# A bidirectional scan in 32-token chunks: odd chunks' halves swapped, both directions in one phase, PSUM banks in changing roles

## The reference, cut to what matters

```python
def step(S, inp):
    rt, wt, kt, vt, at, bt = inp
    Sa = jnp.einsum('zbhij,zbhj->zbhi', S, at)
    S = S * wt[..., None, :] + Sa[..., :, None] * bt[..., None, :] + vt[..., :, None] * kt[..., None, :]
    return S, jnp.einsum('zbhij,zbhj->zbhi', S, rt)
...
_, ys = lax.scan(step, S0, xs)
y = (ys[:, 0] + ys[::-1, 1]).transpose(1, 0, 2, 3)
```

## Time and profile before

| | |
|---|---|
| median of 3 runs | 1479.38 us (1470.05 to 1479.9) |
| the profiled execution | 1478.97 us, span 1477.2 us |
| mean granted TensorE clock | 0.96 of 2.4 GHz |
| TensorE busy | 1368.8 us, 93% of the span |
| DVE busy | 878.4 us, 59% |
| ACT busy | 562.9 us, 38% |
| first L893 of the scan to the last L950 | 340.5 to about 642 us |
| L784 | from 92.8 to 277 us |

### The profile page before, as it was taken

One profiled execution on the slowest core, in us unless ns is written; L12 is line 12 of the kernel. 1 busy time (PEld: TensorE's weight loads), 2 busy tenths in 40 slices (PEclk: granted clock), 3 DMA queues, 4 the chain that ended last, 5 costly groups with the idle time before them and its releaser, 6 DMA issues.

```text
span 1477.2 us, 28497 instructions
## 1 busy us (share of the span) xinstructions
PE 1368.8 (93%) x11292; PEld 1092.4 (74%) x11292; DVE 878.4 (59%) x1151; ACT 562.9 (38%) x825; POOL 168.9 (11%) x165
## 2 busy tenths in 40 slices
PE   6999999985898998878978899999999998999996
PEld 2487787874787877756866688888888887888885
DVE  4967767896565676756248755555555563323235
ACT  3725525311565675672114333333333342112121
POOL 1000100220010000021100322222222200000000
PEclk9999999996899998989988999999999999999998
DMA  5046856974566575621410222222222256322113
GB/s 198 19 121 173 199 138 161 219 219 94 147 211 206 152 219 151 184 70 44 156 71 0 86 85 85 85 78 73 80 81 73 84 172 241 114 86 92 46 33 114
DMA packets 154404, 179.51 MB, mean 122 GB/s; under 512 B 61264, under 2 KB 116624, under 8 KB 154352
## 3 DMA queue, kind: packets, MB, share of 16 engines
q1 hardware_dynamic: 141184, 152.69, 35.3%
q10 hardware_dynamic: 9264, 14.19, 3.1%
q0 software_dynamic: 3904, 11.93, 2.6%
HBM read 121.16 MB, written 57.54 MB: 121 GB/s over the span
## 4 chain that ended last, share of the span: by engine, by line
PE 74%; DVE 13%; ACT 5%; DMA 3%; issue 3%; POOL 1%; ACTq 1%; SPq 1%; DVEq 0%; POOLq 0%
PE banks L1041 26%; PE banks L667 16%; PE banks L649 6%; PE banks L1076 4%; PE banks L655 3%; DVE work L1815 2%; DVE work L1811 2%; PE banks L893 2%; PE banks L903 2%; PE banks L926 2%; PE banks L784 2%; DMA work<-in_w_in 2%; PE banks L631 1%; ACT work L1274 1%; PE banks L872 1%
## 5 line engine op out<-in xcount | busy, mean ns | idle before, releaser
L1041 PE MATMUL banks<-op,sw_hi 128*128 128x512 f32 x1176 | 363.6, 390 | 5.2 <-DVE hT L1997 3.5
L1041 PEld LDWEIGHTS banks<-op,sw_hi 128*128 128x128 f32 x1176 | 221.4, 188 | 52.0 <-DVE sw_lo L1610 3.9
L1041 PE MATMUL banks<-op,sw_lo 128*128 128x512 f32 x588 | 229.3, 390 | 0.0
L1947 DVE TENSOR_TENSOR xT<-xT,banks 128x1024 f32<-128x1024 f32 x24 | 29.3, 1221 | 168.3 <-PE banks L667 156.6
L1041 PEld LDWEIGHTS banks<-op,sw_lo 128*128 128x128 f32 x588 | 110.8, 188 | 23.0
L1384 ACT ACTIVATE sw_hi<-work 128x1024 fp32r<-128x1024 f32 (+1 forms) x63 | 75.9, 1204 | 123.8 <-PE banks L1041 111.7
L1610 DVE TENSOR_TENSOR sw_lo<-work,sw_hi 128x1024 fp32r<-128x1024 f32 (+1 forms) x63 | 90.1, 1430 | 39.4 <-ACT sw_hi L1384 39.3
L649 PE MATMUL banks<-ph_hi,pw_hi 128*128 128x512 f32 x272 | 86.8, 401 | 6.4 <-DVE pw_lo L1610 4.0
L649 PE MATMUL banks<-ph_hi,pw_lo 128*128 128x512 f32 x272 | 85.2, 395 | 0.0
L667 PE MATMUL banks<-g_hi,down_hi 128*128 128x512 f32 x256 | 79.6, 393 | 4.4 <-DVE g_lo L1610 4.3
L667 PE MATMUL banks<-g_lo,down_hi 128*128 128x512 f32 x256 | 79.5, 392 | 0.0
(11 more groups left out here) (246 smaller groups left out, 2578.3 us busy)
## 6 DMA issues: line engine op xcount, KB each, us to landing
work<-scan_d SPq DMA_DIRECT2D x32, 768.0 KB, 4.8
work<-in_w_gu SPq DMA_DIRECT2D x88, 256.0 KB, 4.6
scan_d<-work SPq DMA_DIRECT2D x16, 1024.0 KB, 5.6
g_d<-hT SPq DMA_DIRECT2D x22, 512.0 KB, 2.9
scan_d<-work SPq DMA_DIRECT2D x32, 256.0 KB, 6.3
work<-in_w_down SPq DMA_DIRECT2D x16, 512.0 KB, 3.7
work<-in_w_in ACTq DMA_DIRECT2D x15, 512.0 KB, 3.8
work<-g_d SPq DMA_DIRECT2D x15, 512.0 KB, 4.5
```

The costliest lines, as they stand in the source:

```text
L1041: mm = pe.matmul(banks[:, 3 * slot + bank, :], w[:, n, k * P:(k + 1) * P], x[n][:, k, :], start=(opens and k == 0 and p_ == 0), stop=(k == ...
```

## The change

**Odd chunks' halves are swapped.** `half_rows(e, odd)` gives partitions 64 (e xor odd) on. For odd chunks the keys, the gram rows, the v rows and U of head e lie in the other half. The gram matmul of an odd chunk writes across, and chunks alternate between `ps[1]` and `ps[2]`. In DRAM the rows are stored in the swapped order; the stores of v become 8 DMAs of 32 tokens' partitions for each head pair instead of 2.

**Phases merged.** In the first part of X, in U, the state product and Y, the loops are now j, then z, then e, with one wait ahead and one increment behind, so that four matmuls in a row lie in four quadrants of the array. The second part of X keeps z outside.

**Banks.** In even steps XY are banks 0, 1 and US 2, 3; in odd steps the other way round. The first part of X now waits for `S_add` (the previous state product read), U waits for `Y_out`, the previous Y copied.

**Evictions merged.** U's low half (DVE), its high half (ACT), Y's copy, the add and the multiply by `PC` take both directions in one instruction of 512 columns. `PC` of direction 1 is kept in the order of the steps.

**The order of attention's work.** On TensorE, odd steps have two groups of transposes behind X, the third and the first value product behind U, and the other two value products behind Y. On DVE the logits are spread: head 0 behind the even step's U copy, head 1 behind its state update, heads 2 and 3 behind the odd step's X copy; the maxima stand behind the odd step's state update. On ACT the X copy goes ahead of the fourth exponential; of the normalisation one head stands behind U and three behind Y's copy in the even step; `attended` and three exponentials stand behind Y's copy (and behind the squaring, in late steps) of the odd step.

```diff
+        def half_rows(e, odd, at=0, n=64):
+            first = 64 * (e ^ odd) + at
+            return slice(first, first + n)
...
+        def u_rows(slot, rows, cc):
+            return UV[slot].rearrange("p z c j i -> p (z c) (j i)")[rows, cc:4 - cc:3 - 2 * cc, :]
...
-                    sp.dma_start(v_d.rearrange("(b p) n -> p b n", p=P)[:, :, bass.ds((e * NPAIR + j) * HD, HD)],
-                                 vts[:, :, HD * e:HD * e + HD]).then_inc(s["v_stored"], 16)
+                    for m in range(P // C):
+                        tokens, at = slice(C * m, C * m + C), ((e ^ m % 2) * NPAIR + j) * HD
+                        sp.dma_start(v_d.rearrange("(b p) n -> p b n", p=P)[tokens, :, at:at + HD],
+                                     vts[tokens, :, HD * e:HD * e + HD]).then_inc(s["v_stored"], 16)
...
-                        out = ps[1 + c // 16][h, (c % 16) * 64:(c % 16) * 64 + 64]
+                        out = ps[1 + c % 2][half_rows(e, c % 2), (c // 2) * 64:(c // 2) * 64 + 64]
...
+                    XY = [banks[:, 2 * cc + z, 0:NPAIR * HD] for z in range(2)]
+                    US = [banks[:, 2 - 2 * cc + z, :] for z in range(2)]
...
-                    for z in range(2):
-                        c2 = cc if z == 0 else 1 - cc
-                        pe.wait_ge(sz[z]["U_e0"], n + 1)
-                        pe.wait_ge(sz[z]["U_e1"], n + 1)
-                        settled()
-                        for j in range(NPAIR):
+                    pe.wait_ge(s["U_low"], n + 1)
+                    pe.wait_ge(s["U_high"], n + 1)
+                    settled()
+                    for j in range(NPAIR):
+                        for z, c2 in enumerate(c2s):
                             for e in range(2):
-                                h = slice(64 * e, 64 * e + 64)
-                                mm = pe.matmul(US[z][h, 256 + j * HD:256 + (j + 1) * HD],
-                                               BKs[slot][h, z, j, c2 * HD:c2 * HD + HD], UV[slot][h, z, c2, j, :],
+                                mm = pe.matmul(US[z][64 * e:64 * e + 64, 256 + j * HD:256 + (j + 1) * HD],
+                                               BKs[slot][half_rows(e, c2), z, j, c2 * HD:c2 * HD + HD],
+                                               UV[slot][half_rows(e, c2), z, c2, j, :],
                                                start=True, stop=True)
-                        mm.then_inc(sz[z]["S_mm"], 1)
+                    mm.then_inc(s["S_mm"], 1)
...
+                        act.wait_ge(X_mm[1], n + 1)
+                        act.activation(Xs[:, 1], banks[:, 2 * cc + 1, 0:256], ACT.Copy).then_inc(X_out[1], 1)
                         if cc == 0 and behind:
                             exponentials(blk - 1, 1 - g, (3,))
...
+                        act.activation(Ys[q % 2][:, :, :], banks[:, 2 * cc:2 * cc + 2, 0:256], ACT.Copy).then_inc(s["Y_out"], 1)
                         if late and q in (1, 2):
                             y_square(2 * i + (q - 1 - 2 * YT), q - 1)
+                        if cc == 0 and behind:
+                            normalised(blk - 1, 1 - g, (1, 2, 3))
+                        if cc == 1:
+                            if behind:
+                                attended(*((i, 0) if g else (i - 1, 1)))
+                            act.wait_ge(s["nm_ready"], blk + 1)
+                            exponentials(blk, g, (0, 1, 2))
...
+                        dve.wait_ge(s["S_mm"], n + 1)
+                        tt(St[:, :, :, :], S[:, :, :, :], banks[:, 2 - 2 * cc:4 - 2 * cc, 256:512]
+                           .rearrange("p z (j i) -> p z j i", j=NPAIR), ALU.add).then_inc(s["S_add"], 1)
+                        dve.wait_ge(s["S_add"], n + 1 + FREE)
+                        tt(S[:, :, :, :], St[:, :, :, :], PC[:, :, :, bass.ds(n, 1)].broadcast_to([P, 2, NPAIR, HD]), ALU.mult)\
+                            .then_inc(s["S_new"], 1)
+                        if cc == 0:
+                            logits(i, g, (1,))
+                        else:
+                            maxima(i, g)
```

More of the change, by code:

```diff
@@ L543, in _ @@
                         load_weights(slot, 0, a["w_out"][slot])
-                    for z in range(2):
-                        sp.wait_ge(sz[z]["Y_mm"], NC - 2)
-                        sp.wait_ge(sz[z]["S_mm"], NC - 2)
+                    sp.wait_ge(s["Y_mm"], NC - 2)
+                    sp.wait_ge(s["S_mm"], NC - 2)
                     sp.dma_start(gw, a["gate_w"]).then_inc(s["gw_loaded"], 16)
@@ L838, in _, with scores @@
             mm.then_inc(s["vat_mm"], 1)
-            XY = [banks[:, z, 0:NPAIR * HD] for z in range(2)]
-            US = [banks[:, 2 + z, :] for z in range(2)]
-            def scores(i, g, heads, behind):
+            def scores(i, g, heads, behind, later):
                 blk = 2 * i + g
@@ L846, in scores @@
                     e, hh = h % 2, h // 2
-                    if behind and h == heads[0]:
-                        pe.wait_ge(s["pt_out"], 3 * blk - 3 + FREE)
+                    if behind and later and h < 3:
+                        pe.wait_ge(s["pt_out"], 3 * blk - 5 + h + FREE)
                     if behind and h == GH - 1:
@@ L863, in probabilities, with values @@
                     mm.then_inc(s["pt_mm"], 1)
-            def values(i, g):
+            def values(i, g, parts, scored):
                 blk = 2 * i + g
[L867 to L870, removed]
+                if parts[0] == 0:
+                    pe.wait_ge(val_full, 16 * i + 16)
+                    pe.wait_ge(s["sc_out"], scored)
+                    pe.wait_ge(s["o_out"], blk + FREE)
+                for kb in parts:
+                    pe.wait_ge(s["pt_out"], 3 * blk + kb + 1 + FREE)
                     for e in range(2):
@@ L910, in chunk_steps @@
                         pe.wait_ge(qk_full, 48 * i + 48)
-                        scores(i, g, (0, 1), behind)
+                        scores(i, g, (0, 1), behind, not lead)
                     elif behind:
-                        probabilities(*before, 8 * i + 4 * g + 4)
-                    for z in range(2):
[L915 to L923, removed]
+                        probabilities(*before, scored, (0, 1))
@@ new lines, in chunk_steps @@
+                    if lead and q == 0:
+                        pe.wait_ge(scan_full[0], 16 * 10)
+                        pe.wait_ge(s["lw_full"], 16 * (NPAIR + 6))
+                        pe.wait_ge(s["q_stored2"], 16 * 10)
+                    for z in range(2):
+                        pe.wait_ge(X_out[z], n + 1)
+                    pe.wait_ge(s["Y_out"], n + FREE)
+                    settled()
+                    for j in range(NPAIR):
+                        for z, c2 in enumerate(c2s):
@@ L929, in chunk_steps @@
                     if cc == 0:
-                        scores(i, g, (2, 3), behind)
+                        scores(i, g, (2, 3), behind, not lead)
                     elif behind:
-                        values(*before)
-                    for z in range(2):
-                        c2 = cc if z == 0 else 1 - cc
-                        pe.wait_ge(sz[z]["U_e0"], n + 1)
-                        pe.wait_ge(sz[z]["U_e1"], n + 1)
-                        settled()
-                        for j in range(NPAIR):
+                        probabilities(*before, scored, (2,))
@@ L939, in chunk_steps @@
+                        values(*before, (0,), scored)
+                    pe.wait_ge(s["U_low"], n + 1)
+                    pe.wait_ge(s["U_high"], n + 1)
+                    settled()
+                    for j in range(NPAIR):
+                        for z, c2 in enumerate(c2s):
                             for e in range(2):
[L940 to L942 removed]
+                                mm = pe.matmul(US[z][64 * e:64 * e + 64, 256 + j * HD:256 + (j + 1) * HD],
+                                               BKs[slot][half_rows(e, c2), z, j, c2 * HD:c2 * HD + HD],
+                                               UV[slot][half_rows(e, c2), z, c2, j, :],
@@ L953, in chunk_steps @@
                                                skip_group_check=True)
-                        mm.then_inc(sz[z]["Y_mm"], 1)
+                    mm.then_inc(s["Y_mm"], 1)
+                    if cc == 1 and behind:
+                        values(*before, (1, 2), scored)
             with pe.Fori(0, 1) as i:
@@ L959, in _ @@
                 chunk_steps(i, False)
-            probabilities(NC // 4 - 1, 1, 8 * (NC // 4))
-            values(NC // 4 - 1, 1)
+            probabilities(NC // 4 - 1, 1, 8 * (NC // 4), range(3))
+            values(NC // 4 - 1, 1, range(3), 8 * (NC // 4))
             pe.wait_ge(s["gw_loaded"], 16)
             pe.wait_ge(s["o_out"], 2 * NT + FREE)
-            for z in range(2):
-                pe.wait_ge(sz[z]["Y_out"], NC + FREE)
-                pe.wait_ge(sz[z]["S_add"], NC + FREE)
+            pe.wait_ge(s["Y_out"], NC + FREE)
```

(4 more changed lines are left out.)

153 lines of the change are left out of this document (69 added, 84 removed).

## The result

The changed kernel takes **1494.95 us** (median of 4 runs, 1491.5 to 1497.16), the kernel before 1479.64 (4 runs beside it, 1470.05 to 1483.16). The ratio is **1.0116, 95% interval 1.0086 to 1.0146**: slower by 15.3 us, just over the 1% that I set as the bound. Forecast: 1500.

The account below looks back on a forecast made before the run. TensorE's own stream was taken as the bound. 1478.97 + 0 (scan at full clock) + 20 (clock falls) + 1 (gram) = 1500 us; the forecast's own range was 1486 to 1520, the overall range 1470 to 1520.

Parts of the forecast that it names:

- Merged phases: Scan's four merged matmul phases: four quadrants run together, each phase 0.61 us instead of 1.08; bounds 0.61 and 1.08.
- The reading of L689: Four column tiles sharing all array rows, 8 matmuls in 0.64 us, taken as evidence that four quadrants start together.
- Rival B: Scan: quadrants don't run together, merged phases stay 1.08 us, 16.7 us a pair, no gram gain: 1514 us; chance 0.10.
- The hole of 1.8 us before U in each even step: Scan: TensorE idles 1.8 us while maxima, three exponentials and X's copy finish; U begins 4.45 us after S.
- 14.9 us a pair at full clock: Scan: even step 8.5 us plus odd step 6.4 from S to S, against 15.4 a pair before.
- rival C: Scan: TensorE stays the bound, 11.7 us a pair, -59 us: 1420 us; chance 0.08.
- The clock: Scan: half clock after the hole in 13 of 16 pairs, 1.8 us each: +23, less 3; bounds 0 and 40.
- Rival A: Scan: clock holds at full level if holes stay under about 1.4 us; 1477 us, not slower; chance 0.24.
- Scan: +20 expected: Whole scan: about 0 at full clock (-5 + 6), plus 23 for clock falls, less 3 for earlier falls.
- The late iterations: Scan's last three iterations: DVE's centring and ACT's squaring delay the step after q = 1; about +2 us an iteration.
- Gram: Gram products ahead of the scan: -2 us from direction 1, +3 for clock falls (0 to +14), sum +1.
- Stores of v: Ahead of the scan: 8 DMAs a head pair instead of 2 on SP's queue, 0 to +5 us.

Follow-up runs that it names:

- experiment 1: The changed kernel with the four merged phases' loops back in row order z, j, e, at most two quadrants in turn: 1503.74 us, ratio 1.0174.
- experiment 7: experiment 4 with the merged phases' loops in row order z, j, e, two quadrants in turn: 1487.47 us, ratio 1.0067.
- Experiment 4: The changed kernel with the odd step's row maxima moved on DVE from behind the state update to behind U's copy: 1466.68 us, ratio 0.9926.
- experiment 3: The changed kernel with six unread identity products on TensorE behind the even step's scores: 1477.96 us, ratio 1.0013.
- experiment 5: experiment 4 with ACT's squaring in the last three iterations moved behind its other work of the step: 1443.41 us, ratio 0.9767.
- experiment 6: experiment 5 with unread identity products in the late iterations, six before U of q = 2, four before the transposes of q = 3: 1447.43 us, ratio 0.9793.

## Why the prediction was right

The time (1500 for 1494.95) and the mechanism hold: four quadrants shorten the phases, the late maxima and exponentials open a hole, and the clock makes the hole dear. That the sum comes within 5 us is in part luck, since several terms were off and offset each other.

- **Merged phases, 0.61 expected in place of 1.08, the rival 1.08:** 0.69 for L907 as a group, 0.63 from its start to the next phase's. The reading of L689 decided rightly. The Trainium skill ("TensorE: Matmul & The Clock Gate", Part 3, The mechanism) lets a weight load overlap running matmuls only where the row group differs; the same section also names a background weight buffer as a second case, and no run here shows whether that is what is at work. Experiments 1 and 7 speak against the row group as a bound: with two tiles to a row group the phase is 0.69 us, and the same matmuls in row order take 0.97. Rival B is out.
- **The hole of 1.8 us before U in each even step:** 1.81, by the operations named (maxima, three exponentials, copy of X). Experiment 4, which moves only the maxima, removes it.
- **14.9 us a pair at full clock:** 14.79 in experiment 3, where the clock is full and the path the same (from S to S 8.34 us in the even step and 6.45 in the odd one, for 8.5 and 6.4 in the sum; the terms given for 4.45 add up to 4.38 and those for 6.4 to 6.5, which changes nothing); 14.56 in the late pair of the change that no fall meets (7.39 + 7.17). Not 11.7: rival C is out. Its price was right only for TensorE; even without the hole (experiment 4) the pair is 13.4.
- **The clock:** a fall in every steady pair (expected 13 of 16 in all), priced at 1.8, and 16.9 - 14.8 = 2.1 measured, inside the bounds. Rival A is out. Its condition, holes under about 1.4 us, was too simple. In the steady scan every hole of 1.8 us has its fall, and holes of 0.3 us have none (experiments 3 and 4). But holes of 1.25 us have a fall in three of five steady pairs of experiment 1, equal ones of 1.45 us have one or none in experiment 5, and in the change itself the clock stays up behind one of 1.57 us (579.30) and behind those of 1.79 us in the head pairs (150.61). The length of one hole does not decide alone; what else does, no run separates.
- **Scan: +20 expected, +19.4 measured** (table, from its start to the first down product). Its shares were not as summed. The first 11 steps brought -2.7 where the sum has +2 (5.5 pairs x -0.5, and 2.5 falls, if the three pairs without one are here): they wait for loads (L907 for the load of v, 3.4 us), and the kernel before had falls of its own there, for which I took off only 3. Steps 11 to 19: +5.9, as summed (4.5 pairs x 1.3). The late iterations: +12.4, expected +13 (3 x 2, and 5.5 falls x 1.8, less 3 for those of before); the hole before U is 5.1 us there (4.7 by the sum: 1.8 + 2.9). That agreement hides a different make-up: the three iterations bring +8.7, +1.8 and +1.8; the falls are two long ones (20.5 and 23.9 us at half clock), not one in each pair; and a second hole, of 2.70 us ahead of the transposes of q = 3, where ACT's squaring waits for DVE's centring, was not in the sum. The last step and attention: +3.8, not in the sum at all. The clock falls at 636.2 for 34.1 us, over work that does not overlap. But 1.9 of the 3.8 us come from the order: ACT has the last three exponentials behind `attended` now, which waits for the last value products, and so TensorE waits 7.14 us for the last normalisation where it waited 5.24. A term for the tail of the stage was missing.
- **Gram: -2 for the products, +3 for falls.** From each gram's start to that of its transposes, against the kernel before, the products gave nothing in direction 0 and 0.52 us in direction 1 (0.5 expected) in three head pairs, but 0.34 and 1.85 in the last one: 3.8 us in all, since the sum had overlooked that the last pair waits for no further shift. Only one fall, of 3.4 us, came, behind the last pair, so the +3 was too much. The scan starts 2.2 us earlier, not 1 later; that is of the right sign and within the scatter of the start.
- **Stores of v:** 0 taken. The eight stores take 5.67 us from 166.28 (0.71 each), and the gram rows' store follows at 172.00, just as before. In the last pair they take 6.37 us where two took 3.42, and the gram rows' store follows them at once, but it still starts 0.5 us earlier than before and the loads behind it 1.9. No cost is seen; this was not tried by itself.

The chance of 0.55 for slower by over 1% goes with a ratio whose interval (1.0086 to 1.0146) reaches across that bound. Experiment 1 loses only 9 us where B had +14 against the forecast. One part of the reason is measured: B's phases of 1.08 us come out at 0.9 from start to start when the loops are merged but in row order, and so its full-clock pair is 15.9 us, not 16.7. That the denser TensorE keeps the clock up longer fits the rest, but stays open.

## What to carry to other kernels

When a change makes the bounding engine's work shorter by merging, list in order what each of the other engines issues between two uses of a shared result: the work that hid there (here maxima and exponentials ahead of a copy) becomes the path, and moving two such pieces a few lines was worth 51 us (experiment 5), the quadrants by themselves 9 to 21. Price the idle time that a gain leaves on TensorE twice, once as time and once as clock: a short stage of useless products tells in one run which of the two costs. Once the holes are gone there is little left for such filling to win (experiment 6).

## What the runs showed of the hardware

- 64x64 and smaller fp32 tiles in four quadrants run together, two to a row group included: 128 records of gram matmuls in 2.10 us against 3.78 in another order, 32 records in 0.69 us against 0.97.
- In the steady scan one hole of 1.8 us in a pair of steps brought the granted clock to 1.2 GHz for 6.8 us, in pair after pair; six useless 128x128 products in the hole kept it at 2.4 GHz for 89 us and took 17 us from the whole.
- Many small holes did not do what one did: in experiment 4 TensorE idled 8.3 of 73 us in holes of up to 0.3 us, and one of 0.54, and the clock stayed at 1.00.
- A hole's length alone did not tell whether the clock would fall: it stayed at 1.00 behind holes of 1.79 us in the head pairs, and fell behind some of 1.25 us in experiment 1.
